# Making half of one operand of the expert-gate spreading on ScalarE instead of VectorE

## The reference, cut to what matters

```python
ids = i1 * N_KEYS + i2                      # 8 heads x 16 picks = 128 picks of a token
g = jax.nn.softmax(top_s, axis=-1)
act = gelu(einsum('td,tkd->tk', hx, u_tab[ids]))
out = einsum('tk,tkd->td', g * act, v_tab[ids])
```

## Time and profile before

| | |
|---|---|
| device time, median of 3 runs | 3678.66 us (3677.17 to 3678.77) |
| device time of the profiled execution | 3672.6 us |
| span of the profiled execution, first to last instruction | 3671.0 us |
| busy PE, PEld, DVE, ACT, POOL | 87%, 75%, 66%, 28%, 33% |
| mean granted clock of PE, as a share of full speed | 0.934 |
| the three gate stages, in us of the span | about 1378 to 1432, 1516 to 1570, 1655 to 1709 |

### The profile page before, as it was taken

One profiled execution on the slowest core, in us unless ns is written; L12 is line 12 of the kernel. 1 busy time (PEld: TensorE's weight loads), 2 busy tenths in 40 slices (PEclk: granted clock), 3 DMA queues, 4 the chain that ended last, 5 costly groups with the idle time before them and its releaser, 6 DMA issues.

```text
span 3671.0 us, 45673 instructions
## 1 busy us (share of the span) xinstructions
PE 3194.5 (87%) x15833; PEld 2757.7 (75%) x15833; DVE 2425.5 (66%) x3230; ACT 1032.6 (28%) x1447; POOL 1201.0 (33%) x847
## 2 busy tenths in 40 slices
PE   5879975667979986784999999999999999999993
PEld 3667765556754886783778999999999999999993
DVE  1167744454142669777666788777887778877778
ACT  1222142223130233322222333332333323333332
POOL 2376640002420441240111344334443344333440
PEclk9999986668989998997999999999999999999997
DMA  8677730003212424335777888888888888888884
GB/s 308 247 269 292 283 127 0 0 0 110 91 52 99 140 94 153 113 133 204 207 223 218 265 311 285 299 297 302 298 291 303 294 305 296 290 303 301 296 290 162
DMA packets 267968, 784.71 MB, mean 214 GB/s; under 512 B 117616, under 2 KB 125936, under 8 KB 221936
## 3 DMA queue, kind: packets, MB, share of 16 engines
q1 hardware_dynamic: 217328, 476.30, 39.0%
q0 software_dynamic: 45952, 301.09, 22.2%
q10 hardware_dynamic: 4608, 6.29, 0.5%
HBM read 743.76 MB, written 39.85 MB: 213 GB/s over the span
## 4 chain that ended last, share of the span: by engine, by line
PE 57%; issue 26%; POOL 7%; DMA 4%; DVE 4%; ACT 1%; SPq 0%; POOLq 0%; ACTq 0%; PEldq 0%; DVEq 0%
PE ps L1895 28%; PE ps L1822 22%; PE ps L1587 6%; POOL split L702 3%; DMA arena<-in_w_ada 2%; POOL wout_parts L694 2%; DMA arena<-in_w_slices 1%; POOL win_parts L651 1%; POOL win_parts L657 1%; DVE arena L1402 1%; DMA below_parts<-acts_ahead 1%; DVE arena L1399 0%; PE ps L1553 0%; DVE arena L1421 0%; DMA arena<-x_rows 0%
## 5 line engine op out<-in xcount | busy, mean ns | idle before, releaser
L1895 PE MATMUL ps<-split,w_parts 128*128 128x512 f32 x4608 | 1061.9, 390 | 54.5 <-DVE split L1470 35.9
L1822 PE MATMUL ps<-h_parts,split 128*128 128x384 f32 x6144 | 1083.0, 335 | 28.6 <-POOL split L702 28.5
L1822 PEld LDWEIGHTS ps<-h_parts,split 128*128 128x128 f32 x6144 | 1070.1, 188 | 38.4 <-issue 31.2
L1895 PEld LDWEIGHTS ps<-split,w_parts 128*128 128x128 f32 x4608 | 864.4, 188 | 238.8 <-DVE split L1470 37.0
L993 ACT ACTIVATE split<-below_parts 128x1024 fp32r<-128x1024 f32 x448 | 475.6, 1062 | 1297.5 <-PE ps L1895 740.5
L1470 DVE TENSOR_TENSOR split<-below_parts,split 128x1024 fp32r<-128x1024 f32 x448 | 548.7, 1225 | 397.3 <-ACT split L993 393.3
L714 POOL COPY arena<-arena 128x1 uint32 x256 | 186.9, 730 | 1067.7 <-DVE arena L1445 542.2
L702 POOL TENSOR_TENSOR split<-below_parts,split 128x1024 fp32r<-128x1024 f32 x64 | 176.2, 2755 | 416.5 <-ACT split L957 416.5
L1445 DVE SCALAR_TENSOR_TENSOR arena<-arena 128x2048 f32<-128x2048 f32 x128 | 300.4, 2347 | 2.7 <-DVE arena L1437 2.3
L1426 DVE CUSTOM_DVE_ANT_0 arena<-arena 128x2048 f32<-128x2048 f32 x128 | 292.3, 2283 | 0.0
L717 POOL DMA_INDIRECT arena<-in_v_tab,arena x128 | 238.4, 1863 | 110.0 <-POOL arena L714 101.9
(11 more groups left out here) (255 smaller groups left out, 2863.4 us busy)
## 6 DMA issues: line engine op xcount, KB each, us to landing
below_parts<-in_u_units SPq DMA_DIRECT2D x256, 512.0 KB, 4.6
below_parts<-in_v_tab SPq DMA_DIRECT2D x256, 512.0 KB, 6.7
arena<-in_w_ada SPq DMA_DIRECT2D x96, 1024.0 KB, 8.0
arena<-in_w_slices POOLq DMA_DIRECT2D x56, 512.0 KB, 4.5
gates_by_expert<-arena SPq DMA_DIRECT2D x24, 1024.0 KB, 3.9
below_parts<-gates_by_expert SPq DMA_DIRECT2D x32, 768.0 KB, 8.8
below_parts<-in_w_out SPq DMA_DIRECT2D x32, 512.0 KB, 3.5
below_parts<-in_w_q SPq DMA_DIRECT2D x16, 512.0 KB, 3.5
```

What stands on the lines that cost most here:

```text
L1822: ins = nc.tensor.matmul(ps[:, 6 + b, 0:DT], lhs[:, cols], h2_parts[:, rhs, k, :], start=k == 0 and n == 0, stop=k == KT - 1 and n == 2)
L1895: ins = nc.tensor.matmul(ps[:, 2 * m + b, :], w_parts[:, buf, lhs, i, m * P:(m + 1) * P], rhs[:, b * 512:(b + 1) * 512], start=i == 0 and ...
```

## The change

In batches 0, 2, 4, ... of a stage the left operands are made by ACT; DVE keeps the right ones, and everything in the odd batches. ACT takes, token by token, the absolute distance |i1 - iota| (`Abs` with scale -1 and the column of i1 as bias), and over the eight tokens at once `Relu(1 - distance)`, which is 1 where the distance is 0 and 0 elsewhere, since distances are whole numbers. Between the two it waits on `hot_near`, its own semaphore, and it raises `hot_first` behind them, for which PE now waits too in even batches. ACT makes the operands of batch b + 2 just before it stages batch b. The staging copies themselves (`staged`, now line 950) are what they were; the loop holds four batches, and the last four stand behind it.

```diff
+            def hot_part(n, b):
+                buf = b % HOTS
+                act.wait_ge(g_ps, n * (OH // 4) + (b + 1) * (OH // 4))
+                for t in range(OH):
+                    at_t = n * OH + b * OH + t
+                    ins = nc.scalar.activation(one_hot[buf][:, 0, t, :], iota[:, :], ACT.Abs, scale=-1.0, bias=pick_cols[:, 0, bass.ds(at_t, 1)])
+                ins.then_inc(hot_near, 2)
+                act.wait_ge(hot_near, n + (b + 2))
+                nc.scalar.activation(one_hot[buf][:, 0, :, :], one_hot[buf][:, 0, :, :], ACT.Relu, scale=-1.0, bias=1.0).then_inc(hot_first, 2)
+
+            def staged(n, b):
+                st = b // 2 % 2
+                if b % 2 == 0:
+                    act.wait_ge(g_stored[st], n * 4 + (16 * (b // 4 + 1)))
+                for q in range(2):
+                    act.wait_ge(g_ps, n * 2 + (HOTS * OH // 4 + 2 * b + q + 1))
+                    nc.scalar.activation(stage[...], wide(4 + q, 4, NKEY).rearrange("p t i -> p i t"), ACT.Copy).then_inc(g_staged, 1)
+
             def gates_by_expert(m):
-                with act.Fori(0, P // (2 * TG)) as i:
...
+                first = m * P // OH
+                act.wait_ge(cols_ready, m + 1)
+                act.wait_ge(sc_ps, TB)
+                hot_part(0, first)
+                with act.Fori(0, 3) as i:
+                    for b in range(4):
+                        if b % 2 == 0:
+                            hot_part(i * 4, first + b + 2)
+                        staged(i * 4, first + b)
+                for b in range(12, 16):
+                    if b % 2 == 0 and b + 2 < 16:
+                        hot_part(0, first + b + 2)
+                    staged(0, first + b)
@@ one_hots, on DVE
-                    nc.vector.tensor_tensor(hot[:, 0, :, :], ..., ALU.is_equal)
+                    if n % 2:
+                        nc.vector.tensor_tensor(hot[:, 0, :, :], ..., ALU.is_equal)
@@ gates_by_expert, on PE
                         pe.wait_ge(hot_ready, i * HOTS + (m * (P // OH) + buf + 1))
+                        if buf % 2 == 0:
+                            pe.wait_ge(hot_first, i * HOTS + (m * (P // OH) + buf + 2))
```

More of the change, by code:

```diff
@@ L460, in decoder_layer @@
             "q8_ready sc_ps sc_ready sc_used pair_sub pair_exp topk_done row_used idx_copied dots_done gelu_done "
-            "x1_moved h2_high h2_split parts_read cols_ps cols_ready hot_ready g_ps g_staged "
+            "x1_moved h2_high h2_split parts_read cols_ps cols_ready hot_near hot_first hot_ready g_ps g_staged "
             "pre_high pre_split pre_used pre_gelu high_done unit_split unit_used tile_gelu w_made w_high w_ready v_read picks_w tail_loaded tail_row tail_row_ready "
@@ L469, in decoder_layer @@
          q8_ready, sc_ps, sc_ready, sc_used, pair_sub, pair_exp, topk_done, row_used, idx_copied, dots_done, gelu_done,
-         x1_moved, h2_high, h2_split, parts_read, cols_ps, cols_ready, hot_ready, g_ps, g_staged,
+         x1_moved, h2_high, h2_split, parts_read, cols_ps, cols_ready, hot_near, hot_first, hot_ready, g_ps, g_staged,
          pre_high, pre_split, pre_used, pre_gelu, high_done, unit_split, unit_used, tile_gelu, w_made, w_high, w_ready, v_read, picks_w, tail_loaded, tail_row, tail_row_ready,
@@ L930, in scores @@
                 nc.scalar.activation(sc, wide(0, 2, PH, NKEY), ACT.Copy).then_inc(sc_ready, 1)
-            def gates_by_expert(m):
-                with act.Fori(0, P // (2 * TG)) as i:
[L935 to L940, removed]
+            def hot_part(n, b):
[7 more added lines that the diff above has]
+                nc.scalar.activation(one_hot[buf][:, 0, :, :], one_hot[buf][:, 0, :, :], ACT.Relu, scale=-1.0, bias=1.0).then_inc(hot_first, 2)
@@ new lines, in staged @@
+            def staged(n, b):
[4 more added lines that the diff above has]
+                    act.wait_ge(g_ps, n * 2 + (HOTS * OH // 4 + 2 * b + q + 1))
+                    nc.scalar.activation(stage[:, st, :, 8 * (b % 2) + 4 * q:8 * (b % 2) + 4 * q + 4], wide(4 + q, 4, NKEY).rearrange("p t i -> p i t"), ACT.Copy)\
+                        .then_inc(g_staged, 1)
@@ L1398, in one_hots @@
                     dve.wait_ge(g_ps, (first + OH) // 4)
-                    nc.vector.tensor_tensor(hot[:, 0, :, :], over(iota[:, :], 1, OH), over(pick_cols[:, 0, first:first + OH], 2, NKEY), ALU.is_equal)
+                    if n % 2:
+                        nc.vector.tensor_tensor(hot[:, 0, :, :], over(iota[:, :], 1, OH), over(pick_cols[:, 0, first:first + OH], 2, NKEY), ALU.is_equal)
                     for t in range(OH):
```

## The result

| | before | after |
|---|---|---|
| device time, median (14 runs each, same chip) | 3678.72 us (3673.5 to 3684.61) | 3688.86 us (3681.89 to 3698.88) |
| ratio, with its 95% interval | | 1.0032 (1.0022 to 1.0042) |
| profiled execution, device time / span | 3672.6 / 3671.0 us | 3689.5 / 3687.9 us |
| mean granted clock of PE | 0.934 | 0.928 |
| gate stages, each and together | 53.89, 53.88, 53.89: 161.7 us | 57.61, 60.98, 55.90: 174.5 us |

The account below looks back on a forecast made before the run. DVE bounds the stages before, ACT after, at 6.76 us for two batches. Stages +6.7 us and low-clock pairs +5.4 us make +12.1 us, 3684.7 us for the profiled execution, 3690.8 us against the median; range 3676 to 3709 us.

Parts of the forecast that it names:

- What bounds the kernel: In the three gate stages DVE sets the pace, 6.37 us for two batches; what DVE alone gains goes into idle time.
- What is added: On ACT, eight distances and a clamp for every two batches: 3.56 us, 3.47 us until the next copy can start.
- Staging, now exposed: On ACT behind each hot part, copies and PE's answer take 3.29 us, making 6.76 us for two batches.
- The sum: Over the three stages, pairs, ACT's entry and slow starts give 168.4 us against 161.7 us, +6.7 us.
- start at 1.2 GHz: In each stage's first pair, PE's two quads at low clock cost 0.9 us more each, 1.8 us.
- The clock inside a stage: PE's longer waits let its clock fall: one further low pair a stage, +5.4 us in all.
- the 0.7 us of ACT's later or earlier entry: At stage starts ACT is free 2.1 us behind DVE's start in the second, 1.4 us ahead in the third: 0.7 us.
- The clock stays up: Rival: PE's clock stays up after each stage's start, +6.7 us, 3685.4 us; chance 0.20.
- The bias column is free: Rival: an ACT distance costs 0.20 us, 17.3 us less in all, 3673.5 us, up to 3679 us; chance 0.12.
- DVE stays the bound: Rival: ACT's hot part takes under 1.95 us, pairs 5.24 us, stages lose 27 us, 3651.5 us; chance 0.03.
- The register instructions are not hidden: Rival: register instructions ahead of 144 of 192 ACT distances make them 0.40 us, 16 us more, 3706.6 us; chance 0.17.
- PE runs low throughout: Rival: PE's clock never recovers in the stages, 1.8 us more in each of 24 pairs, 3723 us; chance 0.05.

Follow-up runs that it names:

- e6: The kernel before without DVE's comparisons of batches 4, 6, ... 14 of each stage, nothing in their place: 3660.92 us, ratio 0.9948 to before.
- e1: The changed kernel with ACT's distances moved between the copies of two batches and the clamp behind them, same work: 3658.45 us, ratio 0.9947 to before.
- e5: The changed kernel with six unused matmuls on PE behind even batches, except in the first and last pair: 3684.27 us, ratio 1.0012 to before.
- e3: The changed kernel with ACT making left operands of batches 0, 4, 8 and 12 only, DVE the rest: 3668.42 us, ratio 0.9969 to before.
- e8: The changed kernel without the clamps and ACT's wait on itself, even batches' left operands staying distances: 3657.40 us, ratio 0.9942 to before.
- e2: The changed kernel with six unused matmuls on PE behind every even batch, first and last pair too: 3687.46 us, ratio 1.0022 to before.

## Why the prediction was right

**What bounds the kernel.** It held. Six comparisons off DVE shorten a stage by 6.8 us, which is 6 x 1.13 us (e6), and DVE's earlier end alone is worth nothing, as its idle time behind `select` shows (22.74 to 31.06 us).

**What is added.** A distance was priced at 0.39 us and a spacing of 0.29 us from line 849: 388 ns, and (2.43 - 0.388) / 7 = 0.29 us. The clamp at 1.06 us took 1.057; ACT's wait on itself, estimated at 0.05 us, took 0.10 (1380.67 + 2.44 to 1383.21 in the first hot part of after). A hot part until the next copy was 3.47 us and is 3.49. (The prediction's terms as printed add up to 3.53 us and not to 3.56; it had reckoned with a spacing of 0.294 us. Nothing hangs on 0.03 us a pair.) The Trainium skill (ScalarE: Activation LUTs, "What ACT_TABLE_LOAD costs") has a formula for such an ACTIVATE with a column as bias, 280 ns and 0.833 ns a column, with neighbours that overlap by 93 ns. An estimate by it for 128 columns is 387 ns, 294 ns apart, and the rows agree (388 ns and 0.29 us).

**Staging, now exposed.** 3.29 us predicted, 3.25 measured; the pair 6.76 against 6.71 to 6.74; the gap of PE "some 2.7" against 2.8. e1 shows that it was the right thing to look at: when it is covered, the pair drops to 5.55 us with the same instructions.

**The sum.** Here two terms were mis-sized, and they cancelled. Each stage's **start at 1.2 GHz** was counted at 1.8 us and cost 0.71, 0.19 and 0.52 us, 1.4 and not 5.4 us together (read off the first pairs against the steady one). **The clock inside a stage** was counted as one low pair of 1.8 us in each stage, 5.4 us; there were two lengthened places in each, by 0.97 and 1.64, 1.58 and 2.74, 1.09 and 1.49 us, 9.5 us. Together 10.9 us where 10.8 had been counted. The steady chain of 3 x 54.1 us, the 0.7 us of ACT's later or earlier entry and these 10.9 us make 173.9 us, and 174.5 were measured. By stage the prediction's own terms give 57.7, 59.8 and 56.3 us against 57.61, 60.98 and 55.90; the 56, 58 and 55 us that it names among its signs leave out the low pair inside each stage. That the total of 12.1 us came within a microsecond of the stages' 12.8 us is in this part luck; the 10.1 us between the medians is as near as their interval (8 to 15 us) can tell.

**The rivals.** *The clock stays up*: no, it fell in every stage, though e5 shows what it would have given (1.0012, 5.5 us between the medians, where the rival said 6.7). *The bias column is free*: no, the spacing is 0.29 us. *DVE stays the bound*: not with a hot part of 3.5 us for every second batch; with one for every fourth it does (e3). *The register instructions are not hidden*: 144 of them, 46 ns each, stand in the rows of line 938, and eight distances take 2.43 us with them and 2.44 without, so they cost nothing. *PE runs low throughout*: no, six places of 24 pairs.

**What stays open.** Why only some gaps of 2.8 us end in a fall: the pairs on both sides of a lengthened one look alike in the rows, and five of the six lengthened ones are the second or the third of their stage. How much of the spread among the 14 runs of after comes from falls in these stages: only one of them has a trace. And whether POOL, a third of whose span is busy, could make the left operands: that was not tried.

## What to carry to other kernels

Before moving work to an idle engine, write down what that engine answers to: here a chain of copies that another engine waits for and answers. The busy share (40%) said there was room, and there was, but only in the places where ACT waited for PE; put there (e1), the same instructions turned 0.3% of loss into 0.5% of gain, and put in one block behind the copies they lengthened the loop by all they cost. When a change turns many short waits of PE into fewer long ones, count the clock too: here it was some 9 of the 12.8 us.

## What the runs showed of the hardware

- PE's clock fell in six places of 24 pairs, with gaps of 2.2 to 2.8 us ahead of the lengthened matmuls (3.9 us of fp32 matmuls in one piece where the clock is up); with the same gaps it stayed at 1.00 from 1412 to 1438 us. Past the start of a stage it did not fall with gaps of 1.59 to 1.73 us (e1, e8), nor before with gaps of 1.14 us. In e5, with fillers of 1.5 us in each gap, it was 0.97 to 1.00.
- Work that nobody reads can pay: 1.5 us of it a pair took 9 us out of the stages (e5). At a low clock (2.16 us in place of 1.50) and ahead of work that is waited for it cost 7.4 us in e2.
- A fall of the clock costs only where PE's answer is on the path: e3's stages have falls and are 49.34, 49.35 and 49.35 us.
- A register instruction (46 ns) ahead of an ACTIVATE of 128 columns is hidden entirely behind the one that runs: eight take 2.43 us with them and 2.44 without.
